# Both prompt attentions: the softmax division as a diagonal in the product that turns the weights

## The reference

```python
# latent attention (causal over 512 keys), q in blocks of 128
s = mla_scores(qn, qp, k_nope, k_pe)            # 128-wide part + 64-wide rotary part, scaled
s = jnp.where(key_pos[None, :] <= q_pos[:, None], s, -jnp.inf)
pr = jax.nn.softmax(s, axis=-1).astype(v.dtype)
o = jnp.einsum('bhqk,bkhd->bqhd', pr, v)
# cross-attention into 256 memory tokens
s = jnp.einsum('bthd,bmhd->bhtm', q, k).astype(F32) * (MEM_HD ** -0.5)
pr = jax.nn.softmax(s, axis=-1).astype(v.dtype)
o = jnp.einsum('bhtm,bmhd->bthd', pr, v).reshape(bsz, t, MEM_DIM)
```

## Time and profile before

| what | value |
|---|---|
| median of 3 runs | 1699.57 us (1697.11 to 1700.07) |
| profiled execution, own time | 1700.4 us |
| profiled execution, span | 1698.6 us |
| PE busy | 1536.2 us (90%) |
| DVE busy | 817.6 us (48%) |
| ACT busy | 616.2 us (36%) |
| latent attention block | about 243 to 305 us of the span |
| cross-attention block | about 1196 to 1228 us of the span |

### The profile page before, as it was taken

The page is one execution under the profiler, slowest core; times in us unless marked ns, Lnnn a source line. Parts: engine busy times, 40 slices in busy tenths (PEclk is TensorE's granted clock), DMA queues, the critical chain, the costliest instruction groups (busy, mean ns, idle before and its releaser), DMA issues. The chain is left out here.

```text
span 1698.6 us, 28700 instructions
## 1 busy us (share of the span) xinstructions
PE 1536.2 (90%) x10236; PEld 1203.3 (71%) x10236; DVE 817.6 (48%) x1663; ACT 616.2 (36%) x1614; POOL 118.2 (7%) x213
## 2 busy tenths in 40 slices
PE   5997968549999999999999959998798999998999
PEld 5897444337777777787777735443536999997998
DVE  6222678665656556565756522333674222225121
ACT  5032223635545555455545410000314333334211
POOL 0000000021111112021211110000000000000000
PEclk8999867769999999999999979999799999999999
DMA  7131000122312213131312036046013333331231
GB/s 238 37 87 36 16 1 1 52 55 66 90 52 75 72 55 86 54 93 49 97 49 78 2 113 216 0 149 223 1 33 93 85 88 99 91 82 57 82 114 45
DMA packets 190592, 127.80 MB, mean 75 GB/s; under 512 B 49240, under 2 KB 176081, under 8 KB 190468
## 3 DMA queue, kind: packets, MB, share of 16 engines
q1 hardware_dynamic: 190476, 126.38, 25.5%
HBM read 120.05 MB, written 6.37 MB: 74 GB/s over the span
## 5 line engine op out<-in xcount | busy, mean ns | idle before, releaser
L1466 PE MATMUL bank<-keys_high,turned 128*128 128x512 f32 x1024 | 355.9, 408 | 0.3 <-DVE turned L1874 0.3
L1648 ACT ACTIVATE arena<-bank 128x512 f32<-128x512 f32 x256 | 153.3, 599 | 253.9 <-PE bank L1466 253.7
L1466 PEld LDWEIGHTS bank<-keys_high,turned 128*128 128x128 f32 x1024 | 192.6, 188 | 51.8 <-issue 4.1
L1874 DVE TENSOR_TENSOR turned<-bank,turned 128x256 fp32r<-128x256 f32 x258 | 109.3, 424 | 222.7 <-ACT turned L1641 222.2
L1466 PE MATMUL bank<-keys_low,turned 128*128 128x512 f32 x512 | 202.0, 394 | 0.0
L1880 DVE TENSOR_REDUCE arena<-arena 128x4 f32<-128x512 f32 x256 | 173.0, 676 | 0.0
L2482 PE MATMUL bank<-h_high,ffn_high 128*128 128x260 f32 x704 | 142.5, 284 | 3.0 <-DVE h_low L2540 3.0
L2482 PE MATMUL bank<-h_low,ffn_high 128*128 128x260 f32 x704 | 142.8, 284 | 0.0
L2482 PE MATMUL bank<-h_high,ffn_low 128*128 128x260 f32 x704 | 142.1, 284 | 0.0
L1956 PE MATMUL bank<-arena,yT 128*128 128x512 f32 (+1 forms) x240 | 119.5, 634 | 3.6 <-DMA arena<-in_w_mix_out 3.2
L2482 PEld LDWEIGHTS bank<-h_high,ffn_high 128*128 128x128 f32 x704 | 109.4, 190 | 3.1 <-issue 3.1
(11 more groups left out here) (464 smaller groups left out, 2717.3 us busy)
## 6 DMA issues: line engine op xcount, KB each, us to landing
arena<-in_cache_mla_ckv SPq DMA_DIRECT2D x256, 128.0 KB, 2.0
arena<-in_ffn_w_gate SPq DMA_DIRECT2D x22, 512.0 KB, 4.0
arena<-in_ffn_w_up SPq DMA_DIRECT2D x22, 512.0 KB, 5.1
arena<-in_ffn_w_down SPq DMA_DIRECT2D x16, 704.0 KB, 4.8
arena<-in_w_in SPq DMA_DIRECT2D x16, 512.0 KB, 3.9
arena<-in_cache_mla_kpe SPq DMA_DIRECT2D x256, 32.0 KB, 1.8
arena<-in_x_prompt SPq DMA_DIRECT2D x8, 512.0 KB, 6.8
arena<-in_w_mix_out SPq DMA_DIRECT2D x2, 2048.0 KB, 10.4
```

Source lines behind the costliest of these rows:

```text
L1466: last = nc.tensor.matmul(bank[2 + n % 2][:], t[:, (2 * part + k) * P:(2 * part + k + 1) * P], w[wpart][:, k, :], start=(m == 0), stop=(m ...
L1648: nc.scalar.activation(square[n % 2], keys[:], ACT.Square)
L1874: nc.vector.tensor_tensor(t[:, KL:2 * KL], bank[n % 2][:, 0:KL], t[:, 0:KL].bitcast(F32), ALU.subtract).then_inc(p_e, 1)
```

## The change

DVE no longer scales the item's weights. It scales the 128x128 identity by the reciprocals of the row sums into a new buffer `inv` (three of them), which gives a diagonal matrix for the item. PE then turns the weights with a float32 product against this diagonal, weights as the stationary and the diagonal as the moving operand, in place of a transpose against the identity. The product gives the transposed weights already divided. The reciprocal, ACT's steps, the scores and the values are as before. Before it writes a diagonal again, DVE waits until the turning that read the buffer's last content, three items earlier, has been done. Each engine issues as many instructions as before at the level of the program, in the same order; two of them have other operands.

```diff
@@ -855,6 +855,7 @@
         n_items = len(items)
         prob = at(base, 3, 512)
         probT = at(base + 1536, 2, 512)
+        inv = at(base + 2560, 3, P)
         nbias, total = stats[:, 0:3], stats[:, 3:6]
@@ -887,7 +888,8 @@
                         if m >= 2:
                             pe.wait_ge(a_pte, m - 1)
                         for kt in range(keys_of(items[m][1])):
-                            last = nc.tensor.transpose(bank[3 + m % 2][:, kt * P:(kt + 1) * P], prob[:, m % 3, kt * P:(kt + 1) * P], ident)
+                            last = nc.tensor.matmul(bank[3 + m % 2][:, kt * P:(kt + 1) * P], prob[:, m % 3, kt * P:(kt + 1) * P], inv[:, m % 3, :],
+                                                    start=True, stop=True)
                         last.then_inc(a_pt, 1)
@@ -946,10 +948,11 @@
                     m = n - 1
                     if 0 <= m < n_items:
-                        nk = keys_of(items[m][1]) * P
                         dve.wait_ge(a_exp, m + 1)
                         st(nc.vector.reciprocal(total[:, m % 3:m % 3 + 1], total[:, m % 3:m % 3 + 1]))
-                        nc.vector.tensor_scalar(prob[:, m % 3, 0:nk], prob[:, m % 3, 0:nk], total[:, m % 3:m % 3 + 1], None, ALU.mult).then_inc(a_pn, 1)
+                        if m >= 3:
+                            dve.wait_ge(a_pt, m - 2)
+                        nc.vector.tensor_scalar(inv[:, m % 3, :], ident, total[:, m % 3:m % 3 + 1], None, ALU.mult).then_inc(a_pn, 1)
```

## The result

The changed kernel takes 1706.45 us, the median of 12 runs (1701.97 to 1708.18), against 1699.32 us of 12 runs of the kernel before. The forecast was 1705.2 us, 5.6 us slower. The profiled execution took 1707.98 us, with a span of 1706.2.

What follows compares the result with a forecast made beforehand. A closed loop through DVE and PE (scaling, turning, values, copy out) was taken as the bound. Latent attention 3.0, cross-attention 2.9, loads 0.75, less 1.0 for the clock, gave 5.65 us: 1705.2 us, range 1700.8 to 1709.0.

Steps and rivals of the forecast that it cites:

- The loop: Both attention blocks: scaling, turning, values, copy out, next scaling set the item's period, 1.73 us in cross-attention.
- The price of a pass: PE's turning: a float32 product's second pass adds 0.11 us per key tile, 0.21 at the half clock.
- The load: First weight load of each turning: 0 to 0.05 us more exposed in some 30 items; half taken, 0.75 us.
- DVE: Scaling in both blocks: always 128 columns, 286 ns, saving 1.6 us in latent attention and 1.1 in cross-attention, 2.7 in all.
- The added wait: DVE's scaling waits for the turning three items earlier: claimed to cost nothing.
- Cross-attention, 2.9 us: Cross-attention block's added time: 0.7 at the start, 2.0 over 13 full-clock periods, 0.2 for the last turning.
- What follows the blocks: Parts after the attention blocks: taken as unchanged; the prediction is wrong if they take up the blocks' delay.
- Latent attention, 3.0 us: Latent attention's added time by key tiles turned: 0.6, 0.6, 0.7 and 1.2 us for one to four tiles.
- The clock's part: Latent attention: the full clock comes some 3 us sooner, from about 270, giving back about 1.0 us.
- A much sooner clock: Rival, latent attention: full clock by about 256, kernel about 1702.5 us; chance 0.15.
- The hidden passes: Rival: second pass fits PE's idle time, DVE sets the pace, only its 2.7 us remain, 1696.9 us; chance 0.12.
- The dearer passes: Rival: load exposed 0.05 us at some 65 tiles, 3.3 us, perhaps no sooner clock; 1706.2 to 1708.8 us; chance 0.16.

Runs made afterwards that it cites:

- The change's two halves: Kernel before with only PE's product turning, 1708.36 us; kernel before with only DVE's scaling narrowed to 128 columns, 1696.12 us.
- cutting the loop: Reciprocal and scaling moved ahead of the copy out on DVE: 1683.8 us in the kernel before, 1688.91 us in the changed kernel.
- after again: The changed kernel run once more, unaltered, for a second profile: 1705.93 us, ratio 1.0032 to the kernel before.
- filled tail: The changed kernel with two unused float32 products in each of PE's last two idle stretches in latent attention: 1705.69 us, ratio 1.0039.
- the single-pass product: The changed kernel with weights and diagonal in rounded float32, one turning record per key tile: 1702.95 us, ratio 1.0019 to the kernel before.

## Why the prediction was right, step by step

The forecast's number came out, and the loop under it is shown. But that the sum came so close is in part luck: several of its terms were off by more than the 1.0 us that it missed by, and they cancelled.

*The loop.* Right. The change's two halves gave the periods 2.00 and 1.66, and cutting the loop took 14 us off the kernel before and hid the second pass from the cross-attention's period (1.36 us with and without it). The kernel after waited for L902 in each item, 9.1 us in 13 waits instead of 7.1 in 14:

```profile
DVE yT L946 <- PE bank L902: 9.1, 13, 0.7
```

*The price of a pass.* Right: 0.11 us at the full clock, from 0.44 to 0.71 us for two more records, with 0.05 for the load. The load was mis-sized. I took half of 0 to 0.05 us; it was the whole 0.05, so the period is 1.93 and not 1.88. By itself that is 0.75 us more than the sum had.

```profile
L891 PEld LDWEIGHTS bank<-arena x144: 186/192/338, 249.5 to 1238.4; 128*128 128x128 f32 x144
```

*DVE.* Right: 0.286 us in all 32 items, and the narrower scaling alone gave 2.7 us. That this is the sum's figure to the tenth is chance: its interval is 0 to 5.3 us, and the blocks in its profile gave 0.2 and 2.2 us where the sum had 1.6 and 1.1. *The added wait.* Right: no wait of L955 for a turning is listed in either block.

*Cross-attention, 2.9 us, or 3.3 with its half of the loads.* Changed alone, the block grew by 2.9 (31.7 to 34.6), with the whole load in each of its periods. The periods at the full clock added some 0.2 us each, as they should, and the start and the end of the block less than the sum's 0.7 and 0.2: the full clock lasted past the block's end, where before it ended at 1225.5. In the whole change the block grew by 1.7, since the full clock came 3.1 and not 5.8 us into it.

*What follows the blocks.* The sum took the parts behind as unchanged, and the prediction named it as a sign of being wrong if they took up the delay. Behind the cross-attention they did: 3.9 us less in the mean of three profiles, more than the 1.6 that the block grew by, with a half clock of 3.4 us in place of 10.2 or 13.6. Between the blocks it went the other way, 3.4 us more. The two cancel, which nothing in the prediction foresaw.

*Latent attention, 3.0 us plus half of the loads, less 1.0 for the clock.* At like clocks the change cost 3.8 us there, the passes with the loads' whole price. The clock's part was wrong for the profiled execution: the rise came at 274.8. In three other profiles with the change in that block (after again, filled tail, latent attention alone) it came 26.6 to 26.7 us into it, the sooner rise that I had in mind, but so it did once with the old form. What I had not seen is the half clock in the tail, 1.5 us in one profile of the changed kernel and over 2 in the other. The block grew by 5.1 us in the mean of three profiles, where the sum had 2.4.

*The rivals.* A much sooner clock did not come in any profile. The hidden passes are refuted for this order of DVE's work; in the other order they hold for the cross-attention's period. The dearer passes were the right direction for the load alone. The Trainium skill ("TensorE: Matmul & The Clock Gate", "Part 4: PE-mode transpose") says that transposes do not bring the full clock on as other PE work does. By that rule products in place of transposes should bring it sooner, and no run here supports it: with the single-pass product it came 39.7 us into the block instead of 30, and transposes alone went along with its rise in the earlier trace rows. In cross-attention it did come after 3.1 us in the whole change, but after 5.9 with only that block changed, much as before.

*What stays open.* The parts that were not changed differ by up to 5 us between executions and forms, why the half clock falls where it does is shown by no run, and the medians of the two single-attention kernels (0.9 and 3.7 us by their ratios) are less than the sums of their blocks. I can't say how much of the 6.6 us is the loop and how much the clock; the blocks at nearly like clocks say 3.8 + 2.9 = 6.7, with the clock's gains and losses elsewhere about even.

## What to carry to other kernels

Find the closed loop of waits that sets the period before pricing an edit; work that is added inside it costs in full, though every engine has idle time, and the same work left the cross-attention's period as it was when the loop was cut. Look first for an instruction that an in-order engine issues behind a wait it doesn't need: to move the division ahead of the copy out was worth 14 us, where the change under study fought over tenths within that loop. And compare stages at like clocks, and look behind the changed block as well as in it: here the full clock outlasted the changed cross-attention, and the unchanged part behind it gave back more than the block had lost. A total that fits can hide two such errors.

## What the runs showed of the hardware

A turning by a product of the rounded float32 form took as long as a transpose, 0.44 us for two records at the full clock. The granted clock fell to half in latent attention's tail while PE still had turnings and values to do, after an idle stretch of 2.1 us; in the kernel before it stayed full over two such stretches of 2.3 us. With 1.9 us of unused products in each of these stretches it stayed full in the one profile taken. Behind the cross-attention's full clock the half clock was 3.4 or 3.5 us long in all three profiles of the changed form, and 10.2 or 13.6 us in those of the form before.
